# A four-block transformer kernel: two gate products placed inside the state-space core of the first layer

## What is computed

```
proj = x @ w_in                       # 12 tiles of 128: xm (4), zm (4), us (4)
xc   = silu(causal_dwconv(xm))        # 4 taps
q, k = blocks of 4 of xc;  v = blocks of 4 of xm
gates = concat(q, k, v) @ w_if + b_if
h    = mlstm_chunkwise(q, k, v, gates)
out_m = (norm(h) * mh_gain + skip * xc) * silu(zm)
y    = gelu(s5_ssm(us, ...))          # 32 groups of 16 inputs, 64 complex states
out_s = y * sigmoid(y @ w_glu + b_glu)
out  = concat(out_m, out_s) @ w_out
```

## Time and profile before

| what | us |
|---|---|
| median of 3 timed runs | 2554.01 (2550.05 to 2554.66) |
| the profiled execution, its own time | 2550.76 |
| span of the profiled execution | 2548.9 |
| PE busy | 2434.8 (96%) |
| VectorE busy | 1482.4 (58%) |
| ScalarE busy | 1078.3 (42%) |

### The profile page before, as it was taken

One profiled execution on the slowest core, in us unless ns is written; L12 is line 12 of the kernel. 1 busy time (PEld: TensorE's weight loads), 2 busy tenths in 40 slices (PEclk: granted clock), 3 DMA queues, 4 the chain that ended last, 5 costly groups with the idle time before them and its releaser, 6 DMA issues.

```text
span 2548.9 us, 33196 instructions
## 1 busy us (share of the span) xinstructions
PE 2434.8 (96%) x11659; PEld 1971.2 (77%) x11659; DVE 1482.4 (58%) x2175; ACT 1078.3 (42%) x1411; POOL 159.4 (6%) x156
## 2 busy tenths in 40 slices
PE   8987999999989998999999989999999989999999
PEld 6755778888778877888887767788888767788887
DVE  7855465442367754544425586687732676687732
ACT  5333343342356554433324373454422464455421
POOL 1010110000010002000002011000001011000000
PEclk9887899999999999999999899999999999999999
DMA  7311123333322212333333201233333211233331
GB/s 170 83 50 34 51 82 99 92 94 99 95 58 74 80 52 66 115 92 97 91 99 99 70 21 52 83 105 99 93 93 110 83 34 42 77 109 94 95 99 62
DMA packets 400935, 209.78 MB, mean 82 GB/s; under 512 B 18083, under 2 KB 397623, under 8 KB 400855
## 3 DMA queue, kind: packets, MB, share of 16 engines
q1 hardware_dynamic: 397111, 199.65, 27.2%
q0 software_dynamic: 3408, 9.02, 1.4%
q10 hardware_dynamic: 336, 0.05, 0.0%
HBM read 204.49 MB, written 4.19 MB: 82 GB/s over the span
## 4 chain that ended last, share of the span: by engine, by line
PE 87%; DVE 6%; ACT 3%; issue 2%; DVEq 1%; DMA 0%; ACTq 0%; SPq 0%
PE bank L657 68%; PE bank L693 4%; PE bank L1202 2%; PE bank L697 2%; DVEq L1763 1%; DVE w_lo L1734 1%; DVE small L2487 1%; ACT w_hi L1276 1%; PE bank L1178 1%; PE bank L1153 1%; PE bank L1074 1%; PE bank L900 1%; PE bank L939 0%; PE bank L835 0%; PE bank L723 0%
## 5 line engine op out<-in xcount | busy, mean ns | idle before, releaser
L1734 DVE TENSOR_TENSOR w_lo<-w_raw,w_hi 128x1024 fp32r<-128x1024 f32 x380 | 475.6, 1252 | 629.2 <-ACT w_hi L1276 623.6
L657 PE MATMUL bank<-h_hi,w_hi 128*128 128x512 f32 x1864 | 737.2, 396 | 4.2 <-DVEq L1763 3.9
L657 PE MATMUL bank<-h_lo,w_hi 128*128 128x512 f32 x1864 | 727.0, 390 | 0.0
L657 PE MATMUL bank<-h_hi,w_lo 128*128 128x512 f32 x1864 | 726.9, 390 | 0.0
L1276 ACT ACTIVATE w_hi<-w_raw 128x1024 fp32r<-128x1024 f32 x380 | 401.7, 1058 | 666.5 <-PE bank L657 649.7
L657 PEld LDWEIGHTS bank<-h_hi,w_hi 128*128 128x128 f32 x1864 | 351.2, 188 | 82.3 <-issue 9.2
L657 PEld LDWEIGHTS bank<-h_hi,w_lo 128*128 128x128 f32 x1864 | 351.1, 188 | 74.5 <-issue 3.2
L657 PEld LDWEIGHTS bank<-h_lo,w_hi 128*128 128x128 f32 x1864 | 350.7, 188 | 74.0
L657 PE MATMUL bank<-hid_hi,w_hi 128*128 128x512 f32 x704 | 273.9, 389 | 0.0
L657 PE MATMUL bank<-hid_hi,w_lo 128*128 128x512 f32 x704 | 273.9, 389 | 0.0
L657 PE MATMUL bank<-hid_lo,w_hi 128*128 128x512 f32 x704 | 273.9, 389 | 0.0
(11 more groups left out here) (454 smaller groups left out, 2851.6 us busy)
## 6 DMA issues: line engine op xcount, KB each, us to landing
w_raw<-in_ffn_w SPq DMA_DIRECT2D x120, 512.0 KB, 3.8
w_raw<-in_w_up SPq DMA_DIRECT2D x88, 512.0 KB, 3.8
w_raw<-in_c_w_in SPq DMA_DIRECT2D x32, 512.0 KB, 4.1
w_raw<-in_w_down SPq DMA_DIRECT2D x32, 512.0 KB, 3.9
w_raw<-in_w_in SPq DMA_DIRECT2D x28, 512.0 KB, 3.8
w_raw<-in_w_o SPq DMA_DIRECT2D x16, 512.0 KB, 3.9
w_raw<-in_ab_w_in SPq DMA_DIRECT2D x12, 512.0 KB, 6.9
w_raw<-in_ffn_w SPq DMA_DIRECT2D x16, 384.0 KB, 3.3
```

What stands on the lines that cost most here:

```text
L657: mm = nc.tensor.matmul(out[:], w[:, s, k], v[:, kt], start=(kt == 0 and w is w_hi and v is hi), stop=(kt == sum(slabs) - 1 and v is lo))
L1734: nc.vector.tensor_tensor(w_lo[:, s], w_raw[:, s], w_hi[:, s].bitcast(F32), ALU.subtract).then_inc(lo_done, 1)
```

## The change

It has six parts.

1. On PE the last two tiles of w_in (`product(h_hi, h_lo, [KD], 2)`) move from the end of `project` into `s5_core`, between the last `swap_inputs` and the first `swap_sums`. `swap_sums(i)` now waits for quarter i, where PE had waited once for all four. `swap_inputs(i)` uses bank (i + 2) mod 4.
2. On ScalarE the two `gate_in` behind L843 move behind the four copies to `s5_state`.
3. `s5_state` and `s5_z` share a new buffer `s5_pair`, quarter by quarter, over the memory of `s5_in` (quarter i of `s5_in` has been read when quarter i is written). `s5_w` lies in `tmp`. `lstm_bd` goes to the second half of `h_lo`.
4. VectorE's two splits move from ahead of the core to between `turn_and_sum` and `turn_back`.
5. The lower bounds are cut in two: the three operations ahead of the Exp stand behind `convolve`, the rest behind `lstm_heads`. ScalarE's Exp moves into `lstm_gates`, behind another Exp. Their 32 columns are now `small[:, 208:240]`.
6. The multiplication of `s5_sin` by `sign` (128 x 2048) goes. Instead `es`, from which the table is built, is multiplied before the loop (128 x 32). Each doubling carries the sign on, since sign x sign is 1.

```
         u_step = m("u_step", [P, GROUPS, CH], 16)
-        s5_state = hm("s5_state", [P, GROUPS, CH], 8)
-        s5_w = hm("s5_w", [P, GROUPS, CH], 16)
-        s5_z = hm("s5_z", [P, GROUPS, CH], 24)
+        s5_pair = m("s5_pair", [P, 4, 2, GROUPS // 4, CH], 24)
+        s5_state, s5_z = s5_pair[:, :, 0], s5_pair[:, :, 1]
+        s5_w = tmp[:].rearrange("p t (g c) -> p t g c", c=CH)
...
-        lstm_bd = m("lstm_bd", [P, 4, 4, P], 24)
+        lstm_bd = hm("lstm_bd", [P, 4, 4, P], 24)
...
                     nc.tensor.matmul(out[:], shifted[:, off:off + P], s5_k.rearrange("p g w -> p (g w)"),
                                      start=True, stop=True).then_inc(prep["pe_to_scalar"], 1)
-                product(h_hi, h_lo, [KD], 2)
...
                 def swap_inputs(i):
-                    out = take(i)
+                    out = take((i + 2) % 4)
...
                 swap_inputs(3)
-                pe.wait_ge(s5["vector_to_pe"], n(s5["vector_to_pe"], 4))
+                product(h_hi, h_lo, [KD], 2)
                 for i in range(4):
+                    pe.wait_ge(s5["vector_to_pe"], n(s5["vector_to_pe"]))
                     swap_sums(i)
...
                                          ACT.Copy).then_inc(bank_free[5 + j % 3], 1)
-                for t in (2, 3):
-                    gate_in(t)
-                act.wait_ge(hgrn["vector_to_scalar"], n(hgrn["vector_to_scalar"]))
-                nc.scalar.activation(small[:, 0:16], small[:, 0:16], ACT.Exp).then_inc(hgrn["scalar_to_vector"], 1)
...
+                for t in (2, 3):
+                    gate_in(t)
                 for i in range(4):
                     act.wait_ge(s5["pe_to_scalar"], n(s5["pe_to_scalar"]))
                     nc.scalar.activation(ys_step[:, 8 * i:8 * i + 8], bank[i][:].rearrange("p (g c) -> p g c", g=8),
...
                 nc.scalar.activation(r[3], r[2], ACT.Exp, scale=-1.0).then_inc(scalar_step, 1)
+                act.wait_ge(hgrn["vector_to_scalar"], n(hgrn["vector_to_scalar"]))
+                nc.scalar.activation(lb_row[:, 0:16], lb_row[:, 0:16], ACT.Exp).then_inc(hgrn["scalar_to_vector"], 1)
                 act.wait_ge(scalar_step, n(scalar_step))
...
                 for _ in range(3):
                     square()
+                ts(es, es, sign, -1.0, ALU.mult, ALU.mult)
                 step(nc.vector.memset(s5_cos[:, :, 0:1], 1.0))
...
-                ts(s5_sin[:], s5_sin[:], sign, -1.0, ALU.mult, ALU.mult)
-                settle()
...
                 for i in range(4):
                     turn_and_sum(i)
+                only_split(2)
                 for i in range(4):
                     turn_back(i)
...
                 s5_prepare()
-                only_split(2)
-                lower_bounds()
                 at["bank"] += 12
                 s5_core()
                 lay_out()
                 convolve()
+                lower_exponents()
                 s5_gelu()
                 lstm_gates()
                 s5_glu()
                 lstm_heads()
+                lower_bounds()
                 leave(1)
```

More of the change, by code:

```diff
@@ L243, in program @@
         gate_w = s5_v[:].rearrange("p v g -> p (v g)")[:, 0:12 * GATE_COLS].rearrange("p (k g) -> p k g", k=12)
+        lb_row = small[:, 208:240]
         s5_ldt = small[:, 152:152 + GROUPS]
@@ L844, in project @@
                                      start=True, stop=True).then_inc(prep["pe_to_scalar"], 1)
-                product(h_hi, h_lo, [KD], 2)
             def s5_core():
                 def flat(t, i):
-                    return t[:, 8 * i:8 * i + 8].rearrange("p g c -> p (g c)")
+                    return t[:, i].rearrange("p g c -> p (g c)")
                 def enter(i):
@@ L1340, in leave, with gate_in @@
                 deviation()
+            def gate_in(t):
+                slab()
+                b = turned_bank()
+                nc.scalar.activation(zs[:, t], bank[b][:], ACT.Silu).then_inc(bank_free[b], 1)
             def project():
@@ L1403, in s5_core @@
                     act.wait_ge(s5["pe_to_scalar"], n(s5["pe_to_scalar"]))
-                    nc.scalar.activation(s5_state[:, 8 * i:8 * i + 8], bank[4 + i][:].rearrange("p (g c) -> p g c", g=8),
+                    nc.scalar.activation(s5_state[:, i], bank[4 + i][:].rearrange("p (g c) -> p g c", g=8),
                                          ACT.Copy).then_inc(s5["scalar_to_pe"], 1)
+                for t in (2, 3):
+                    gate_in(t)
                 for i in range(4):
@@ L2067, in turn_and_sum @@
                     settle()
[L2068 to L2070 removed]
+                    for g in range(8):
+                        step(nc.vector.tensor_tensor_scan(s5_z[:, i, g], s5_r8[:, 8 * i + g:8 * i + g + 1].to_broadcast([P, CH]),
+                                                          s5_w[:, i, g], 0.0, ALU.mult, ALU.add))
                     flag(s5["vector_to_pe"])
```

41 lines of the change are left out of this document (18 added, 23 removed).

## The result

| | before | after |
|---|---|---|
| median of 20 runs, us | 2550.3 (2546.66 to 2554.66) | 2554.06 (2550.45 to 2556.05) |
| span of the profiled execution | 2548.9 | 2553.6 |
| PE busy | 2434.8 | 2444.0 |

The ratio is 1.0014 (95% interval 1.0008 to 1.0021): the change makes the kernel 3.8 us slower, where 8.6 us less were forecast. The base of the forecast was also some 2 us high: over 20 runs the kernel before has 2550.3, not the 2552.4 that was put in.

What follows compares the result with a forecast made beforehand. PE was taken as the bound, standing still 9.82 us for VectorE. The second k-step 8.8 us earlier, less 0.2 for the moved Exp, gave 8.6 us: from a base of 2552.4 to 2543.8 us, range 2539 to 2549.

Steps and rivals of the forecast that it cites:

- What bounds the kernel: PE carries 87% of the chain; its 9.82 us hole ahead of the swaps of sums waits for VectorE.
- The parts up to leave 0: Core entry from 103.1, products end 125.1, first quarter 110.7, turn back 129.1, leave 0 at 131.6 instead of 140.44.
- a new hole of 2.9 us: PE idle between swaps of sums and leave 0; clock loss put at 2.0 us, ends nothing and 2.6.
- Rival 3: Core entry's small matmuls run at the lower clock, 22 us; turn back 1.5 us later, about 2552; chance 0.06.
- ScalarE's part: Behind the leaves: last copy until 148.6, first Silu at 148.7, PE starts L900 at 149.4 instead of 157.59.
- VectorE's floor: LSTM front: VectorE's second pair ends at 152.5, so PE's second k-step starts at 154.3 at the earliest.
- the missing table load: ScalarE's load ahead of Silu at 155.57, 1.28 us, goes because the Exp has moved.
- the 8.8 us of the front: PE's second k-step of L900 in the LSTM front starts at 154.9 against 163.73, 8.8 us earlier.
- The covered transfer of ys: ys goes out and back behind the leaves; h_lo ready at 175.4, 1.3 us before PE asks.
- rival 1: 200 to 300 us: mean clock moves by 0.05, 5.5 us come or go, 2549 or 2538; chance 0.13.
- The one that forecast slower: 200 to 300 us: mean clock falls; at 0.65 more than 0.2% slower, about 2558; chance 0.03.
- The rule on the free-running monitor: The clock gate's monitor does not start anew with the kernel, so the point of transition moves between runs.

Runs made afterwards that it cites:

- the run that fills the hole: Changed kernel plus four extra 512-column matmuls on PE just ahead of leave 0, results unused: 2545.02 us against 2550.2, ratio 0.9974.
- the changed wait: Kernel before, with PE waiting for each quarter's scans ahead of its swap of sums, not once for all four: 2563.74 us against 2550.2, ratio 1.0044.
- the sign alone: Kernel before with part 6 only (`es` multiplied by `sign`, the 2048-column operation gone): 2550.18 us, ratio 0.9994.
- the bounds alone: Kernel before with part 5 only (lower bounds cut and moved, with their own columns): 2549.59 us, ratio 0.9995.
- the kernel with two extra matmuls: Changed kernel, VectorE's two splits behind the convolution, two extra 512-column matmuls ahead of leave 0: 2541.12 us, ratio 0.996; again 2541.15 us, ratio 0.9964.
- late splits: Changed kernel with VectorE's two splits behind the turn back instead of ahead of it: 2546.22 us against 2550.2, ratio 0.9982.
- product between the swaps: Changed kernel, splits behind the convolution, second moved product between the third and fourth swaps of sums, no extra matmuls: 2541.39 us against 2550.98, ratio 0.9959.
- the run without filler: Changed kernel with VectorE's two splits behind the convolution, no extra matmuls: median 2550.16 us (2537.37 to 2552.18), ratio 0.9986.
- the extra matmuls behind leave 0: Changed kernel with four extra 512-column matmuls between leave 0 and leave 1: 2548.99 us against 2550.2, ratio 0.9994.

## Why the prediction was wrong

**What bounds the kernel: right.** The hole, its releaser and the way VectorE and PE had waited for each other are as read, and the moved products removed that wait.

**The parts up to leave 0: right.** Counted from the end of the L843 matmuls, the first quarter was forecast at 7.6 us and came at 8.8, the end of the products at 22.0 (21.4), the turn back at 26.0 (27.1) and leave 0 at 28.5 (29.4). The second split had 3.3 us of slack behind ScalarE's w_hi (123.86) in place of 1.7. The new hole was forecast at 2.9 us and is 3.52.

**The step that failed: "Between 128.7 and 131.6 PE has a new hole of 2.9 us. What does it cost?"** The hole was seen, and the clock's fall too. Its price was taken as 2.0 us, with 2.6 as the upper end, from the times after which the clock came back behind the two holes of the trace (4.0 and 5.2 us). It is 27.5 - 14.4 = 13.1 us. With it the second k-step comes 64.2 us behind the L843 matmuls where 51.8 were forecast, 12.4 us late, and that is also the distance between 8.6 us faster and 3.8 us slower. Both those holes were followed by matmuls of 512 columns, the swaps of sums and the LSTM front. What now follows the hole are matmuls of 64 columns, and behind them the clock does not come back at all while they run. The price of a hole was read as a time, though the rows show it only for one kind of work behind it. The rows needed stood there: before, the leaves began at 140.44, and the clock had come back at 138.9, during the swaps. The range's upper end rested on the same rows, so it fell with them. Rival 3 asked whether the small matmuls of the entry would run at the lower clock, but not those of the leaves.

**Behind it.** With the clock held (the run that fills the hole) the second k-step came at 51.9 us behind the L843 matmuls, forecast 51.8: ScalarE's part, VectorE's floor and the missing table load were right, and the 8.8 us of the front were there to be had. The covered transfer of ys was covered: h_lo is ready at 185.11 and PE ends L911 at 187.17. The lower bounds fit into VectorE's wait: 2.26 us of it are left behind them, ahead of the next split.

**The sum beyond the front: short by 3 to 4 us.** The same run was 8.7 us early at the second k-step but only 5.2 us under the kernel before. From that k-step to the reciprocal of the norm the traces fall in three groups. It takes 158.1 to 158.4 us where the lower bounds stand in their old place (before, the changed wait, the sign alone); 159.6 to 160.2 in six traces with the bounds moved, the bounds alone among them (the kernel with two extra matmuls has 160.2 both times, on two chips); and 162.1 to 162.4 in three (four fillers, late splits, product between the swaps). In these last three PE is busy 140.1 to 140.4 us in this stretch at a mean granted clock of 0.84, in the middle group 136.5 to 136.9 at 0.87. So about 2 of the 4 us go along with the clock, which is rival 1 in kind; the other 1.2 to 2.1 go along with the moved lower bounds, which the forecast had priced at 0.2. How the bounds would cost this stays open, and most kernels have a single trace.

**The rivals.** The one that forecast slower put it in the stretch of the heads, at a mean clock under 0.69; measured over 200 to 300 us is 0.80, so its sign was right and its place wrong. The clock was the right resource in three of the four rivals, and in none at the right place. The rule on the free-running monitor of the Trainium skill, "TensorE: Matmul & The Clock Gate", Part 1, is in line with the two groups of the run without filler, of which one execution has a trace; it was weighed for the size of a loss that it does not set.

## What to carry to other kernels

A hole on PE is to be priced by what runs directly behind it: the time from the trace in which the clock came back holds only for the work that stood there. When work is moved into a hole, look at the holes that it leaves, and put the long matmuls last, directly ahead of the short ones, as the real product ahead of the fourth swap does. And PE work that starts earlier is no gain by itself: changing one wait so that the swaps ran earlier, one by one, made the kernel before 11 us slower (7 to 15).

## What the runs showed of the hardware that was not expected

- Unbroken matmuls of 64 columns did not bring the clock up from 0.50: 27 us after and with the changed wait, 22 us without filler. Directly behind matmuls of 512 columns and at 1.00 they kept it: 14 us before and in all four traces with a filler, of extra or of real matmuls.
- The clock can fall behind a hole when work has already resumed. In the execution without filler there were 1.25 us without work, then 64-column matmuls, and the fall some 2.8 us after they began (the clock is 1.00 up to 131.5); with the extra matmuls behind leave 0 the hole was 2.96 us and the fall came 1.2 us after work resumed.
- One and the same kernel, with a 1.25 us hole at such a place, had executions of 2537 and of 2552 us. Three or four runs of it would have told either story.
